# Two attention streams of each layer woven into one block, and norms and a bias table moved into the key-scoring block, on Trainium2

## What is computed

```python
def stick_breaking_block(q, k, v, q_pos, k_pos):            # layer 0, 8 heads x 64
    logit = einsum('bqhd,bkhd->bhqk', q, k) * HEAD_DIM ** -0.5
    before = k_pos[None, :] < q_pos[:, None]
    log_keep = where(before, log_sigmoid(-logit), 0.0)
    log_between = cumsum(log_keep, axis=3, reverse=True) - log_keep
    w = where(before, exp(log_sigmoid(logit) + log_between), 0.0)
    return einsum('bhqk,bkhd->bqhd', w, v)

def dsa_attend(q, k_sel, v_sel, q_pos, idx, rel_bias):      # layer 1
    logit = einsum('bqhd,bqkhd->bhqk', q, k_sel) * HEAD_DIM ** -0.5
    dist = q_pos[None, :, None] - idx
    bias = moveaxis(rel_bias[t5_bucket(dist)], -1, 1)
    p = softmax(where((dist >= 0)[:, None], logit + bias, -inf))
    return einsum('bhqk,bqkhd->bqhd', p, v_sel)

# layer 1, ahead of it: q = rmsnorm(q, dsa_q_norm_g); k = rmsnorm(k, dsa_k_norm_g)
# idx = top_k(einsum('bqh,bqhl->bql', iw, relu(einsum('bqhd,bld->bqhl', iq, ik))), 256)
```

## Time and profile before

| | us |
|---|---|
| median of 3 runs (5516.73 to 5526.84) | 5521.59 |
| the profiled execution | 5522.32 |
| its span in the trace | 5520.7 |
| PE busy | 4248.7 (77%) |
| DVE busy | 2389.5 (43%) |
| ACT busy | 1101.7 (20%) |
| POOL busy | 979.5 (18%) |

### The profile page before, as it was taken

One profiled execution on the slowest core, in us unless ns is written; L12 is line 12 of the kernel. 1 busy time (PEld: TensorE's weight loads), 2 busy tenths in 40 slices (PEclk: granted clock), 3 DMA queues, 4 the chain that ended last, 5 costly groups with the idle time before them and its releaser, 6 DMA issues. The chain is left out here.

```text
span 5520.7 us, 56273 instructions
## 1 busy us (share of the span) xinstructions
PE 4248.7 (77%) x21425; PEld 3301.4 (60%) x21425; DVE 2389.5 (43%) x3646; ACT 1101.7 (20%) x2150; POOL 979.5 (18%) x569
## 2 busy tenths in 40 slices
PE   7756749778799978799707866787176876999799
PEld 6534534336799956577603245677054445999667
DVE  3067640212555521210036567777596133655410
ACT  1123220110111122111014421121153201111121
POOL 2000000000122223222022338000001110222133
PEclk9855656889799989899755567878588987999899
DMA  3211010453211122222133320000413532111220
GB/s 126 72 26 23 12 30 8 134 172 88 63 46 46 38 64 70 78 98 75 51 122 104 111 77 27 28 28 3 131 37 95 159 119 76 50 46 46 64 67 31
DMA packets 239659, 377.87 MB, mean 68 GB/s; under 512 B 106923, under 2 KB 113852, under 8 KB 238079
## 3 DMA queue, kind: packets, MB, share of 16 engines
q1 hardware_dynamic: 213462, 285.77, 17.0%
q0 software_dynamic: 26000, 89.51, 5.3%
HBM read 292.93 MB, written 88.98 MB: 69 GB/s over the span
## 5 line engine op out<-in xcount | busy, mean ns | idle before, releaser
L91 PE MATMUL ffn_up_hp<-ffn_up_xT,ffn_up_w_high 128*128 128x352 f32 x4224 | 1017.1, 324 | 9.5 <-DVE ffn_up_xT L198 9.5
L91 PEld LDWEIGHTS ffn_up_hp<-ffn_up_xT,ffn_up_w_high 128*128 128x128 f32 x4224 | 737.5, 190 | 11.4 <-DVE ffn_up_xT L198 11.4
L91 PE MATMUL ffn_up_hp<-ffn_up_xT,ffn_up_w_low 128*128 128x352 f32 x2112 | 680.7, 322 | 0.0
L91 PEld LDWEIGHTS ffn_up_hp<-ffn_up_xT,ffn_up_w_low 128*128 128x128 f32 x2112 | 399.7, 189 | 0.0
L91 PE MATMUL ffn_down_acc<-ffn_down_w_high,ffn_down_a_high 128*128 128x512 f32 (+1 forms) x792 | 324.5, 410 | 84.3 <-DVE ffn_down_w_low L752 55.1
L91 PE MATMUL od_in_acc<-od_in_w_high,od_in_xT 128*128 128x512 f32 (+3 forms) x1152 | 353.7, 388 | 1.0 <-POOL od_in_w_low L273 1.0
L474 POOL TENSOR_TENSOR ffn_up_w_low<-ffn_up_w,ffn_up_w_high 128x1024 fp32r<-128x1024 f32 x88 | 211.3, 2401 | 760.3 <-DVE ffn_up_w_high L84 760.3
L91 PE MATMUL ffn_down_acc<-ffn_down_w_low,ffn_down_a_high 128*128 128x512 f32 (+1 forms) x792 | 319.5, 403 | 0.0
L91 PE MATMUL ffn_down_acc<-ffn_down_w_high,ffn_down_a_low 128*128 128x512 f32 (+1 forms) x792 | 318.2, 402 | 0.0
L728 POOL TENSOR_TENSOR ffn_down_a_low<-ffn_act_actT,ffn_down_a_high 128x768 fp32r<-128x768 f32 (+2 forms) x144 | 213.2, 1481 | 504.5 <-ACT ffn_down_a_high L700 504.5
L551 ACT ACTIVATE ffn_up_hb<-ffn_up_hp 128x352 f32<-128x352 f32 (+1 forms) x264 | 101.1, 456 | 884.2 <-PE ffn_up_hp L91 884.2
(11 more groups left out here) (589 smaller groups left out, 7915.8 us busy)
## 6 DMA issues: line engine op xcount, KB each, us to landing
ffn_up_w<-ffn_w_in POOLq DMA_DIRECT2D x88, 512.0 KB
ffn_down_raw<-ffn_w_out SPq DMA_DIRECT2D x44, 512.0 KB, 3.9
sbs_pages<-cache_sb_k SPq DMA_DIRECT2D x64, 256.0 KB, 3.0
sbs_pages<-cache_sb_v SPq DMA_DIRECT2D x64, 256.0 KB, 2.9
rwkv_arrays<-rwi_out SPq DMA_DIRECT2D x8, 2048.0 KB, 12.6
dsas_pages<-cache_dsa_k SPq DMA_DIRECT2D x64, 256.0 KB, 3.0
dsas_pages<-cache_dsa_v SPq DMA_DIRECT2D x64, 256.0 KB, 2.9
od_in_w<-od_w_in POOLq DMA_DIRECT2D x7, 2048.0 KB, 10.9
```

Source lines behind the costliest of these rows:

```text
L91: last = nc.tensor.matmul(out, a[p], b[q], start=start and i == 0, stop=stop and i == 2)
```

## The change

Five things are done.

- `attentions` weaves prompt and sample attention of a layer into one block. The prompt has 5 PSUM banks (2 for scores, a ring of 3 that now also takes the value products, a unit of their own), the sample 3 (2 for scores and values, 1 for everything turned). The sample's steps begin at 3.0 with a pace of 1.6 for each half of an item's pages.
- The sample's slots hold 4 pages each instead of 8; Q has 32 columns, each item's scores go to 32 partitions of their own; the products with the new keys come once a round.
- In the prompt, `values` and `turn_out` come first in a step; the value bank is copied out by DVE (`keep_out`) instead of ACT; in layer 1 the weights overwrite the scores' tile (`w = ex`), so a row waits until PE has turned the one two tiles before.
- `s5_setup` of layer 0 gets a block of its own, after the attention block.
- `bias_tables` and `qk_norm` become generators and join `keys_and_inputs`; the table works in one PSUM bank and two row buffers, the norms square in place. The sample's index pages take over the tile of the prompt's index queries, and are loaded once these have been turned.

```diff
-def s5_and_attention(nc, A, proj, mix, q_src, k_src, v_src, attention_mix):
+def s5(nc, A, proj, mix):
...
-                weave(a_tensor(pe), m_tensor(pe))
+                weave(m_tensor(pe))
...
-def prompt_attention(nc, ph, A, q_src, k_src, v_src, mix, softmax, NT, pace=1.0):
+def prompt_attention(nc, ph, A, ident, ident_ld, q_src, k_src, v_src, mix, softmax, pace=1.0):
...
-    w = ph.sb("w", [P, 2, SEQ])
+    w = ex if softmax else ph.sb("w", [P, 2, SEQ])
...
-    ps_o = ph.ps("ps_o", [P, NC_COLS])
...
+            if s % QG == 1 and s > QG:
+                values(s // QG - 1)
+            if s % QG == 2 and s > QG:
+                turn_out(s // QG - 1)
             if s + 2 < TILES:
                 scores(s + 2)
...
-                nc.scalar.activation(oT[:, :], ps_o[:, :], ACT.Copy).then_inc(oT_ready, 1)
...
+            nc.vector.tensor_copy(oT[:, :], ps_t[:, u % NT, :]).then_inc(t_free, 1)
...
+    pages = ph.sb("pages", [P, SLOTS, HALF_PAGES, HALF])
...
+    ps_t = ph.ps("ps_t", [P, NC_COLS])
+    ps_s = ph.ps("ps_s", [P, 2, NC_COLS])
...
+    base = lambda r: start + pace * (2 * HALVES + 3) * r
+    k_step = lambda r, g, c: base(r) + pace * (2 * g + c)
+    row_step = lambda r: base(r) + pace * (HALVES + 0.5)
+    w_step = lambda r: base(r) + pace * (HALVES + 1.5)
+    v_step = lambda r, g, c: base(r) + pace * (HALVES + 2.5 + 2 * g + c)
...
+                        at_least(pe, unit_ev, u)
+                        for hp in range(HP):
+                            last = nc.tensor.transpose(ps_t[:, hp * P:(hp + 1) * P],
...
+def attentions(nc, names, A, prompt, sample, softmax, start, pace):
...
+        p_sync, p_tensor, p_scalar, p_vector, p_gpsimd = prompt_attention(nc, ph, A, ident, ident_ld, *prompt, softmax)
+        s_sync, s_tensor, s_scalar, s_vector, s_gpsimd = sample_attention(
+            nc, ph2, A, ident, ident_ld, *sample, softmax, start, pace)
...
+            weave(p_sync(sp), s_sync(sp))
...
+            weave(p_tensor(pe), s_tensor(pe))
...
+            weave(n_sync(sp), i_sync(sp), k_sync(sp), b_sync(sp))
...
+            weave(n_scalar(act), i_scalar(act), k_scalar(act))
...
+        attentions(nc, ("sb", "sbs"), A, (*qkv(ev, cols, prompt), mix[0][prompt, HALF:]),
+                   (*qkv(ev, cols, sample), pages(A["cache_sb_k"]), pages(A["cache_sb_v"]), mix[0][sample, HALF:]),
+                   False, 3.0, 1.6)
+        s5(nc, A5, ev, mix[0])
```

More of the change, by code:

```diff
@@ L1416, in gpsimd @@
         for h in range(HEADS):
-            yield step((h + 1) * PT + 3) + 0.5 * pace
+            yield step((h + 1) * PT + 2) + 0.5 * pace
             if softmax:
@@ L1550, in scalar @@
         weigh(0)
-        for s in range(TILES + 2):
+        for s in range(TILES):
             yield step(s)
@@ L1756, in sample_attention @@
-        block = ph.block()
+    ps_t = ph.ps("ps_t", [P, NC_COLS])
+    ps_s = ph.ps("ps_s", [P, 2, NC_COLS])
+    table_ld = ph.sem("table_ld")
+    ld = ph.sem("ld")
+    new_ld = [ph.sem(f"new_ld{i}") for i in range(2)]
+    page_ld = [ph.sem(f"page_ld{i}") for i in range(SLOTS)]
+    set_up = ph.sem("set_up")
+    qk_tr = ph.sem("qk_tr")
+    q_ready = ph.sem("q_ready")
+    unit_tr = ph.sem("unit_tr")
+    unit_ev = ph.sem("unit_ev")
+    s_mm = ph.sem("s_mm")
+    keep_done = ph.sem("keep_done")
@@ new lines, in sample_attention @@
+    own = ph.sem("own")
+    w_done = ph.sem("w_done")
+    pv_half = ph.sem("pv_half")
+    o_ev = ph.sem("o_ev")
+    out_ready = ph.sem("out_ready")
+    st = ph.sem("st")
+    out_sum = ph.sem("out_sum")
+    inv_done = ph.sem("inv_done")
+    n_ld = 16 * (3 + (G4 if softmax else 1))
+    if softmax:
+        sel_ld = ph.sem("sel_ld")
+    items = [(r, kv, g, c) for r in range(ROUNDS) for kv in range(2) for g in range(G4) for c in range(2)]
+    base = lambda r: start + pace * (2 * HALVES + 3) * r
@@ new lines, in gpsimd @@
+    def gpsimd(pool):
+        if not softmax:
+            return
+        for r in range(ROUNDS):
+            yield row_step(r - 1) + 0.9 * pace if r else start - 3 * pace
+            at_least(pool, w_done, r)
+            for g in range(G4):
+                b = r * G4 + g
+                src = A["sel_sample"][b * DEC_SEQ:(b + 1) * DEC_SEQ, :]
+                for h in range(HEADS):
+                    pool.dma_start(sel[g * R + h * DEC_SEQ:g * R + (h + 1) * DEC_SEQ, :], src).then_inc(sel_ld, 16)
@@ L1783, in _ @@
[L1783 to L1798 removed]
+            sp.dma_start(ident[:, :], A["c_ident"]).then_inc(ident_ld, 16)
@@ new lines, in bias_tables, with sync, vector, tensor @@
+def bias_tables(nc, ph, A, D, near_sample, bank, wide_rel):
+    rel = ph.sb("rel", [REL_BUCKETS, 2, HEADS])
+    diff = ph.sb("diff", [REL_BUCKETS, HEADS])
+    onehot = ph.sb("onehot", [REL_BUCKETS, NEAR])
+    rows = ph.sb("rows", [P, 2, NEAR])
+    ld = ph.sem("ld")
+    own = ph.sem("own")
+    mm = ph.sem("mm")
+    ev = ph.sem("ev")
+    st = [ph.sem(f"st{i}") for i in range(2)]
+    st2 = ph.sem("st2")
+    step = lambda h: 2 + 2 * h
+    def sync(sp):
+        yield 0
+        sp.dma_start(rel[:, 0, :], A["rel_bias"]).then_inc(ld, 16)
+        sp.dma_start(rel[:, 1, :], A["rel_bias"][REL_BUCKETS - 1:REL_BUCKETS, :]
+                     .broadcast_to([REL_BUCKETS, HEADS])).then_inc(ld, 16)
+        sp.dma_start(onehot[:, :], A["c_onehot"]).then_inc(ld, 16)
+        for h in range(HEADS):
+            yield step(h + 1)
+            sp.wait_ge(ev, h + 1)
+            sp.dma_start(D[h], rows[:, h % 2, :]).then_inc(st[h % 2], 16)
+        yield step(HEADS + 2)
+        for i in range(2):
+            sp.wait_ge(st[i], 16 * HEADS // 2)
+        for h in range(HEADS):
+            sp.dma_start(near_sample[h * DEC_SEQ:(h + 1) * DEC_SEQ, :],
+                         skewed(D[h], NEAR_TOP - 256, 256 + DEC_SEQ, DEC_SEQ)).then_inc(st2, 16)
+        yield step(HEADS + 4)
+        sp.wait_ge(st2, 16 * HEADS)
+    def vector(dve):
+        yield 1
+        dve.wait_ge(ld, 48)
+        nc.vector.tensor_tensor(diff[:, :], rel[:, 0, :], rel[:, 1, :], ALU.subtract).then_inc(own, 1)
+        dve.wait_ge(own, 1)
+        nc.vector.tensor_copy(wide_rel, wide(diff[:, :].unsqueeze(2), [REL_BUCKETS, HEADS, P])
+                              ).then_inc(own, 1)
+        for h in range(HEADS):
+            yield step(h)
+            dve.wait_ge(mm, h + 1)
+            if h >= 2:
+                dve.wait_ge(st[h % 2], 16 * (h // 2))
+            nc.vector.tensor_copy(rows[:, h % 2, :], bank[:, 0:NEAR]).then_inc(ev, 1)
+    def tensor(pe):
+        yield 1
+        pe.wait_ge(own, 2)
+        for h in range(HEADS):
+            yield step(h)
+            at_least(pe, ev, h)
+            nc.tensor.matmul(bank[:, 0:NEAR], wide_rel[:, h, :], onehot[:, :], start=True, stop=True
+                             ).then_inc(mm, 1)
+    return sync, tensor, vector, ev
```

781 lines of the change are left out of this document (367 added, 414 removed).

## The result

The changed kernel took 5535.9 us (median of 14 runs, 5529.7 to 5541.9) against 5522.2 for the kernel before: a ratio of 1.0025, with a 95% interval from 1.0017 to 1.0033. It is slower by a quarter of a per cent. The forecast was 5400, with a range of 5265 to 5510, and a chance of 0.10 for slower. The profiled execution has a span of 5533.0 us, 12.3 more than before.

The account below looks back on a forecast made before the run. No single engine was taken to bound the kernel; merged attention was reckoned by PE's work and waits. Gains of 48 (layer 0), 28 (layer 1) and 45 (key scoring) sum to 121: 5522.3 - 121 = 5401, say 5400 us, range 5265 to 5510.

Parts of the forecast that it names:

- Key scoring: Key-scoring block with norms and bias table inside: 395 + 6 + 30 = 431 us for 476, a gain of 45.
- Set-up alone: Layer 0's state-space set-up in its own block, without cover: 145 us, between 130 and 165.
- Merged attention: Prompt and sample attention woven into one block per layer, work on PE: 473 us in layer 0, 458 in layer 1.
- the four phases of layer 0: Sample key and value phases in layer 0's merged block: 25.6 key steps of 8.6 us, 220; value steps of 5.6, 143.
- the clock of 0.9: TensorE's granted clock expected in the merged blocks, making prompt work on PE 2.9 us a tile.
- The starts: Loads and first weights at the opening of the merged blocks: 31 us in layer 0, 43 in layer 1.
- the prompt's own pace: The 13 merged steps without sample work: about 5.3 us each in layer 0 (69), 3.7 in layer 1 (48).
- leave prompt waits on PE, for which I take 0.4 a step: Merged blocks: the ring of 3 holding value sums and output copies on DVE leave PE 0.4 us of waits a step.
- the clock falls: Rival, chance 0.09: one-bank hand-offs keep TensorE's clock at 0.65 to 0.68 in both merged blocks, +210 us, 5611.
- the prompt's waits stay: Rival, chance 0.12: weights still come late in the merged blocks, +77 us in layer 0, +20 in layer 1, 5498.
- Page copies: PE's waits in key steps for ACT to empty the sample's one bank: 1.4 us a step, 36 in each layer.
- is no longer last: Merged blocks: DVE needs 3.5 us a step for the prompt plus under 1 for the rest, so does not bound.

Follow-up runs that it names:

- the run with the streams in turn: The changed kernel with the sample's start at step 69 in place of 3 in both layers, so its work follows the prompt's: 5685.5 us, 1.0301.
- The run with low parts first: The changed kernel with DVE's low parts of the former tile's weights ahead of the next row instead of behind it: 5479.5 us, 0.9927.
- The run with four banks: The run with low parts first, with the sample's turned pages alternating between two banks and the prompt's ring 2 in place of 3: 5415.4 us, 0.9805.
- the output first: The run with four banks, prompt rows loaded first and set-up loads issued early, plus DVE emptying the turned output's bank before the next row: 5384.8 us.
- the finer weave: The run with four banks, each prompt step cut in three on PE and ACT, page turns spread evenly: 5465.7 us, 0.9897.

## Why the prediction was wrong

**Key scoring: right.** 431 us forecast, 431 measured, and the terms hold too: the opening, up to ACT's first instruction on a mixed tile, takes 69 us for 66 before (6 more were forecast), the rest 362 for 329 (30 more were forecast; that share was a guess). Alone it is worth 45 us (5475.8). The 40 table loads are the ones that were counted, nine of them with 0.2 us of idle time ahead of them as before. The drain that the Trainium skill ("ScalarE: Activation LUTs", section "What ACT_TABLE_LOAD costs") adds to each load would have made the gain an estimated 17 us smaller; the trace shows no such idle time.

**Set-up alone: right but for 17 us.** 128 for 145, just under its range. The loads took 35.5 (37 forecast), the chain up to the first turned bank 70 (72), the eight turned banks 6 (7). What was mis-sized is the end, 16 us for 24 + 5: the last eight banks came 1.78 us apart, where the tightest pair in the rows had stood 2.73 apart.

```profile
952.47 0.68 DVE L1001 TENSOR_TENSOR s_T<-s_setup_pst,s_setup_bmask 128x512 f32<-128x512 f32 x1
954.25 0.68 DVE L1001 TENSOR_TENSOR s_T<-s_setup_pst,s_setup_bmask 128x512 f32<-128x512 f32 x1
```

**Merged attention: the step that failed.** The blocks lasted 561 and 511 where 473 and 458 stood in the sum, 88 and 53 more; a block over 520 was the prediction's own sign of being wrong. For the four phases of layer 0 the forecast was 220 + 143 = 363; they took 438. PE's work at full clock was 287 us, 319 at the clock of 0.9 that I took, for the 307 in the sum: 12 of the miss. The clock made 361 of the 319: 42. PE stood 77 us for the 56 reckoned: 21. In layer 1 the same reckoning gives 0 for the work, 15 for the clock and 7 for waits, of 23. The starts came as forecast: the first weights stand 31 and 44 us into the blocks, for 31 and 43.

```profile
294.19 0.29 DVE L1587 TENSOR_TENSOR sb_w<-sb_cp 128x128 f32<-128x128 f32 x1
...
3986.15 0.40 ACT L1520 ACTIVATE dsa_ex<-dsa_ex,dsa_stat 128x128 f32<-128x128 f32 x1 [2.47 <-DVE dsa_stat L1573]
```

The rest is the steps without a key or value phase beside them, with the tail: 92 us for 79 in layer 0 and 81 for 52 in layer 1, which I had taken from the prompt's own pace before. In layer 1 the prompt's own pace had fallen, as the run with the streams in turn shows (325 us for 264).

Two sentences of the working carry this. *"leave prompt waits on PE, for which I take 0.4 a step"*: that is 20 us a layer, and the waits for DVE's low parts alone were 41.4 in layer 0. I saw that the ring now held the value sums and that DVE copied them, and priced the copies at their own 0.69 us. I did not ask what stood behind them in DVE's queue, nor which of DVE's instructions releases a bank. The run with low parts first takes 41.4 us of such waits down to 6.9 by that order alone; the copy on DVE alone costs 48 us in layer 1's unwoven prompt. *"at the clock of 0.9 that I expect"*: the sample blocks of before ran at 0.91 with PE busy 80%, and I carried that to a mixture whose waits were up to 5 us long. The rival "the clock falls" had the direction, at 0.65 and a price of 210; it came to 0.76 to 0.84 in layer 0 and to 57 us in both layers. It laid the fall to the one-bank hand-offs. The run with four banks bears that out in layer 1; in layer 0 the first rise of the clock came with the ring's release. The rival "the prompt's waits stay" named the low parts, at 77 and 20 us; PE stood 21 and 7 us longer than reckoned. The clock of the same phases rose with the waits at the PSUM banks gone: from 0.76 to 0.88 in layer 0, and from 0.82 to 0.95 in layer 1. The rule of the Trainium skill that stood beside the clock's rival, "TensorE: Matmul & The Clock Gate", section "A second HAM failure mode: psum-queue depth-cycling", points the same way.

**The wait that was foreseen.** Page copies: 1.4 x 25.6 = 36 us in each layer, measured 36.5 and 51.2, so it was right in layer 0 and 15 us short in layer 1. In part that is luck: 45 hand-offs of 0.8 us were reckoned, and 39 waits of 0.94 us were measured in layer 0. Taking the one bank away was worth 64 us.

**DVE "is no longer last".** By busy time that is so, 250 of 511 us in layer 1. But DVE's row is a link of the chain that PE waits on, and three experiments each lost 31 to 50 us with at most 9 us of added work on DVE in a block: the copy on DVE and the output first by a wait put ahead of the row, the finer weave, as I read it, by scores that come later. Not every such wait costs: in layer 0 the output first left the block as it was.

What stays open: which activity of PE makes the chip grant the lower clock. Two phases with the same 33 us of idle time ran at 0.75 and 0.84, so the sum of idle time does not decide it; the waits at the PSUM banks went together with the lower clock in two comparisons, which is not a proof that they, or their length, decide. What makes the gap of 9.7 us behind layer 1's merged block is open too.

## What to carry to other kernels

When a copy is moved to another engine, price the wait that moves with it and what is queued behind it there: 16 copies of 0.69 us cost 48 us in a block where DVE was busy 81%. When two streams are woven, first price what each gives up for it (banks, buffers, cover for a third), here about 100 us a layer against 76 gained. An engine's wait in front of TensorE can cost more than its length, so the largest waits by name are worth removing even where the busy share looks high.

## What the hardware showed that was not expected

- Two phases of one execution, with the same work and the same 33 us of idle PE, differed by 11 us through the granted clock alone (0.75 and 0.84).
- Removing 23 us of PE's waits shortened PE's busy time by another 34 us at unchanged work.
- The second half of B (128 KB), issued right behind the first, kept SP for 17.0 us; issued among the pages of the merged block, 9 us behind the first, it kept SP for 0.44 us, and the block was none the longer (467 and 463 us).
- A fourth PSUM bank in layer 1's prompt ring made no difference (0.9997), while the sample's second bank, with a ring of 2 for the prompt, was worth 26 and 25 us in the two key phases of layer 1 (121 to 95, 123 to 98).
